# Twenty-four V rows go from VectorE to ScalarE and GpSimd, and the gate round moves from row 84 to row 90

## The chip, the cores and the metric

One core of a Trainium2 chip runs the whole layer. The metric is the device time of one execution in microseconds (us). The kernel is written by hand, engine by engine: TensorE (PE in the profile, PEld its weight loads), VectorE (DVE), ScalarE (ACT), GpSimd (POOL) and the sync engine (SP), each with its own instruction stream, tied to the others by semaphores.

## The reference

Input x is 512 tokens of width 1024, float32. A first sub-layer mixes tokens (a gated MLP group and a retention group, one output projection, LayerNorm). The second is a product-key retrieval over 16384 single-neuron experts, and it is where the change lies:

```python
def _peer(h, w_q, sub_keys, u_tab, v_tab):
    ...
    # 8 heads, 16 experts each: 128 experts for every token
    best_s, best_pos = lax.top_k(cand_s, PEER_TOPK)
    gates = jax.nn.softmax(best_s.astype(jnp.float32), axis=-1)
    ...
    def block(args):
        xt, it, gt = args
        act = jax.nn.gelu(jnp.einsum('td,ted->te', xt, u_tab[it]), approximate=False)
        return jnp.einsum('te,ted->td', gt * act, v_tab[it])
```

So for each token 128 rows of the table U give 128 dot products with h, these go through gelu and are multiplied by the gates, and the 128 rows of the table V with the same indices are summed with these weights. Then follow the residual and the second LayerNorm.

## The kernel before

**Two ways for the experts.** The 512 tokens are four tiles of 128. Tiles 0 and 1 are *gathered*: for each of 8 heads and 16 chosen experts there is one U row and one V row for each of the 128 tokens, fetched by indirect DMA. That is 256 gathered rows in all (tile 0: rows 0 to 127, tile 1: 128 to 255), in the code `n`; `u = n // 16` is the unit (tile and head) whose indices and weights a row uses. One row is a 128x1024 float32 tile, 512 KB. Tiles 2 and 3 are *dense*: TensorE multiplies them with the whole tables, streamed from memory by SP in pairs of blocks of 1 MB (`load_pair`), 64 pairs of U and 64 pairs of V.

**The row loop.** VectorE's stream is one loop over `n` from 0 to 287. At each `n` it does, in this order: the choices of experts due at this `n` (`chosen_before`), the gate round if `n` is `ROUND_ROW`, the one-hots of a *team* of 16 dense tokens if one is due (`team_rows_of`), the product of a dense block with its gates (`gated_gelu`), the dot product of U row `n` (`product_row`, L1177), and the add of V row `n-32` (`add_row`, L1200), which multiplies it by its weight and adds it to the sum of its tile, `acc_rows[t]`. GpSimd's loop has the same `n`: it issues the gather of U row `n` (`gather_u`, L606) and then that of V row `n-32` (`gather_v`, L618). There are six buffers for U rows and six for V rows. So `gather_u(n)` waits until VectorE has done dot product `n-6`, and `gather_v(n)` until V row `n-6` has been added. GpSimd works in order, so a wait of either gather holds the other stream too.

**TensorE's order** is a list (`static_jobs`): first the projections and the mixing, then the queries and key scores up to about 408 us, then the first half of the dense U table in 32 steps (`act`, r = 0; 6.91 us each; ScalarE takes each result from one of four PSUM banks with a gelu), then the *gate round* (32 small groups whose one-hots VectorE and ScalarE make, and whose results VectorE multiplies in), then the first half of V (`expert`, r = 0), in the second half of which the teams (1, 0, m) are interleaved, the second half of U (`act`, r = 1), with the teams (1, 1, m) between its first 16 steps, and the second half of V (`expert`, r = 1).

**What ties the two.** `ROUND_ROW` says at which row VectorE enters the gate round, and the rows of the teams are counted from it: team m of (1, 0) at `ROUND_ROW + 31 + m*15//8`, team m of (1, 1) at `ROUND_ROW + 61 + m*15//8`, the product of block k at `ROUND_ROW + 61 + (k+2)*15//8`. The choices of units 7 to 12 have rows of their own (`LATER_CHOICES`); those of the other gathered units come at `n % 16 == 2`, so that of unit 13 at row 178. At row 160 tile 0 gets its LayerNorm (`finish`).

**The end.** Eleven of the last V rows (229, 231, ..., 249, `TAIL_ROWS`) are added by TensorE, once it has finished the dense experts (`s_vdone`): ScalarE first takes the statistics of tiles 2 and 3 from PSUM, then makes diagonals from the weights (L825). Row 235 can be gathered only when row 229 has been added so. VectorE does the dense statistics at row 264, the dense outputs at row 270, then adds the rows from 240 on and normalises tile 1.

## Time and profile before

| | |
|---|---|
| time, median of 3 runs | 1466.14 us (1464.67 to 1469.86) |
| the profiled execution: its own time | 1468.57 us |
| its span, first to last instruction | 1466.6 us |
| PE busy | 1367.8 us (93%) |
| DVE busy | 1144.3 us (78%) |
| ACT busy | 397.9 us (27%) |
| POOL busy | 663.7 us (45%) |
| TensorE clock granted, mean | 0.975 of full speed |

Busy shares are averages over stages that have different limits, so the stage must be read, not the share. In a timeline a row is one instruction or several equal ones: start, duration, engine, line, operation, tiles, count, and in brackets how long the engine had been idle before it and who ended the wait. `big` holds the gathered rows, `y` the sums. "DMA share" is how busy the 16 DMA engines are on average; about 1.0 with 410 GB/s and more is all that is seen in this trace.

### The profile page before, as it was taken

How to read it: one execution, taken by the hardware profiler on the slowest of the kernel's cores; microseconds unless marked ns; L12 is line 12 of the kernel's file. 1: busy time of each engine (PE TensorE's matmuls, PEld its weight loads, DVE VectorE, ACT ScalarE, POOL GpSimd, SP SyncE). 2: the span in 40 equal slices, each digit the busy share in tenths (PEclk: the TensorE clock that was granted, in tenths of full speed). 3: DMA queues.
4: the chain of work that ended last, by engine and by line, in shares of the span. 5: the costliest groups of instructions: out<-in, count | busy, mean ns of one | idle time of the engine just before them, and what ended most of it. 6: DMA issues, size and time to landing. Idle time of an engine off the chain costs nothing.

```text
span 1466.6 us, 18813 instructions
## 1 busy us (share of the span) xinstructions
PE 1367.8 (93%) x6494; PEld 957.1 (65%) x6494; DVE 1144.3 (78%) x2495; ACT 397.9 (27%) x815; POOL 663.7 (45%) x548
## 2 busy tenths in 40 slices
PE   8999989799999999989999599999999999999943
PEld 6787755488888888867544255578888854444411
DVE  4837266678888888789889998878999887666786
ACT  4224000512120101269410055566551010000020
POOL 2334111353333345620335565645445565666673
PEclk9999999999999999999999799999999999999986
DMA  6411234577878889982599999999899999999996
GB/s 237 151 59 58 91 139 144 187 239 235 314 268 310 291 308 414 414 333 77 185 390 397 401 381 413 403 353 398 336 363 353 414 413 414 414 414 414 412 328 257
DMA packets 118429, 444.26 MB, mean 303 GB/s; under 512 B 11712, under 2 KB 24512, under 8 KB 101952
## 3 DMA queue, kind: packets, MB, share of 16 engines
q0 software_dynamic: 73728, 268.47, 48.1%
q1 hardware_dynamic: 44032, 173.56, 30.9%
q8 instruction: 51, 0.84, 0.2%
q10 hardware_dynamic: 576, 1.05, 0.2%
q14 instruction: 42, 0.34, 0.1%
HBM read 440.94 MB, written 2.10 MB: 302 GB/s over the span
## 4 chain that ended last, share of the span: by engine, by line
DVE 32%; PE 30%; DMA 16%; POOL 7%; issue 6%; DVEq 5%; ACT 4%; ACTq 1%; SPq 0%
DMA big<-in_peer_v_dram,idx 11%; DVE y L1200 8%; PE ps L1441 7%; PE ps L1387 7%; DVE big L1177 7%; PE ps L1370 6%; DMA big<-in_peer_u_dram,idx 4%; POOL big L618 4%; POOL big L606 3%; PE ps L1534 2%; PE ps L1625 2%; DVE work L1060 2%; ACT wr L668 1%; DVE topi L1059 1%; DVE top L1062 1%
## 5 line engine op out<-in xcount | busy, mean ns | idle before, releaser
L606 POOL DMA_INDIRECT big<-in_peer_u_dram,idx x256 | 311.9, 1218 | 537.3 <-DVE dots L1177 430.0
L1177 DVE CUSTOM_DVE_ANT_0 big<-big,xh 128x1024 f32<-128x1024 f32 x256 | 311.7, 1224 | 64.5 <-DMA big<-in_peer_u_dram,idx 42.4
L1200 DVE SCALAR_TENSOR_TENSOR y<-big,wgt,y 128x1024 f32<-128x1024 f32 x245 | 314.1, 1282 | 48.9 <-DMA big<-in_peer_v_dram,idx 45.4
L618 POOL DMA_INDIRECT big<-in_peer_v_dram,idx x256 | 290.7, 1136 | 108.2 <-issue 67.1
L1441 PE MATMUL ps<-big,pool_mem 128*128 128x512 f32 x512 | 224.3, 593 | 0.0
L1370 PE MATMUL ps<-xT,big 128*128 128x256 f32 x960 | 211.1, 380 | 0.0
L1370 PEld LDWEIGHTS ps<-xT,big 128*128 128x128 f32 x960 | 181.7, 190 | 24.3
L1441 PEld LDWEIGHTS ps<-big,pool_mem 128*128 128x128 f32 x512 | 96.7, 190 | 118.6 <-issue 118.6
L1441 PE MATMUL ps<-y,pool_mem 128*128 128x512 f32 x256 | 114.8, 599 | 0.0
L1441 PE MATMUL ps<-xT,pool_mem 128*128 128x512 f32 x256 | 113.5, 593 | 0.0
L1370 PE MATMUL ps<-xT,y 128*128 128x256 f32 x480 | 106.4, 380 | 0.0
L1370 PE MATMUL ps<-xT 128*128 128x256 f32 x480 | 106.4, 380 | 0.0
L1370 PE MATMUL ps<-xT,pool_mem 128*128 128x256 f32 (+1 forms) x512 | 102.4, 360 | 2.7 <-ACTq L760 2.4
L1370 PEld LDWEIGHTS ps<-xT 128*128 128x128 f32 x480 | 90.9, 190 | 12.2
L1370 PEld LDWEIGHTS ps<-xT,y 128*128 128x128 f32 x480 | 90.8, 190 | 12.1
L1370 PEld LDWEIGHTS ps<-xT,pool_mem 128*128 128x128 f32 x512 | 88.0, 194 | 13.3 <-issue 3.4
L482 POOL TENSOR_TENSOR weight_parts<-big,weight_parts 128x1024 fp32r<-128x1024 f32 x20 | 49.1, 2474 | 85.5 <-ACT weight_parts L634 85.4
L1441 PEld LDWEIGHTS ps<-y,pool_mem 128*128 128x128 f32 x256 | 48.8, 192 | 59.5 <-issue 59.1
L1441 PEld LDWEIGHTS ps<-xT,pool_mem 128*128 128x128 f32 x256 | 48.3, 190 | 59.3 <-issue 59.3
L676 ACT ACTIVATE sel<-iota,gated 128x128 f16<-128x128 f32 x256 | 83.7, 553 | 0.1
L1387 PE MATMUL ps<-weight_parts,x_hi 128*128 128x512 f32 x320 | 82.8, 404 | 0.8 <-ACT weight_parts L634 0.8
L634 ACT ACTIVATE pool_mem<-ps 128x512 f32<-128x512 f32 (+2 forms) x52 | 28.5, 549 | 181.3 <-PE ps L1370 86.9
(253 smaller groups left out, 1587.9 us busy)
## 6 DMA issues: line engine op xcount, KB each, us to landing
big<-u_pairs_dram SPq DMA_DIRECT2D x32, 1024.0 KB, 8.0
big<-v_pairs_dram SPq DMA_DIRECT2D x32, 1024.0 KB, 8.0
y<-u_pairs_dram SPq DMA_DIRECT2D x16, 1024.0 KB, 7.9
xT<-u_pairs_dram SPq DMA_DIRECT2D x16, 1024.0 KB, 8.1
y<-v_pairs_dram SPq DMA_DIRECT2D x16, 1024.0 KB, 7.9
xT<-v_pairs_dram SPq DMA_DIRECT2D x16, 1024.0 KB, 8.1
big<-in_w_in_dram SPq DMA_DIRECT2D x24, 512.0 KB, 5.8
pool_mem<-in_peer_w_q_dram SPq DMA_DIRECT2D x12, 1024.0 KB, 7.6
```

The lines of the kernel that those rows point to most:

```text
L482: return engine.tensor_tensor(w_lo(g)[:, ks, :], w_full(g)[:, ks, :], w_hi(g)[:, ks, :].bitcast(f32), ALU.subtract)
L606: nc.gpsimd.indirect_dma_start(urow[n % RING], None, peer_u2, bass.IndirectOffsetOnAxis(ap=idx[:, u, e:e + 1], axis=0)).then_inc(s_u[n % R ...
L618: nc.gpsimd.indirect_dma_start(vrow[n % RING], None, peer_v2, bass.IndirectOffsetOnAxis(ap=idx[:, u, e:e + 1], axis=0)).then_inc(s_v[n % R ...
L676: A.activation(ohl[:, t // 4, :, t % 4], iota[:], ACT.Abs, bias=minus_key[:, c:c + 1])
L1060: V.match_replace(spare, values[:, 0:8], src, NEG)
L1177: V.tensor_tensor_reduce(out=urow[n % RING], in0=urow[n % RING], in1=xh[:, u // PH * D:(u // PH + 1) * D], scale=1.0, scalar=0.0, op0=ALU. ...
L1200: V.scalar_tensor_tensor(acc_rows[t], vrow[n % RING], wgt[:, u % 2, e:e + 1], acc_rows[t], ALU.mult, ALU.add).then_inc(s_vadd, 1)
L1370: last = T.matmul(dst, lhs(i), rhs(i), start=(i == 0), stop=(i == n - 1))
L1387: last = T.matmul(dst, *((a, b_) if x_left else (b_, a)), start=(n == 0 and k == 0), stop=(n == 2 and k == KC - 1))
L1441: last = T.matmul(acc[a][:, half * 512:(half + 1) * 512], X[:, i, a * P:(a + 1) * P], rows_v[:, half * 512:(half + 1) * 512], start=False, ...
L1534: T.matmul(bank, mixT[:, k, t * P:(t + 1) * P], w[:, k, :], start=(k == 0), stop=False)
L1625: last = T.matmul(bank[:, t * QUARTER:(t + 1) * QUARTER], hot[:, t // 4 % 2, :, t % 4], ohi16[:, g % 2, t // 4, c, :, t % 4], start=(c == ...
```

## The change

V rows 0 to 23 leave VectorE. For each of them ScalarE multiplies the gathered row in place by its weight (`weighted`), in its stream just ahead of the evacuation of a dense step given by `weighted_behind`; GpSimd then adds it (`pool_add`) into a sum of their own, which lies in `acc_rows[1]`, not yet in use then. At row 124 VectorE adds that sum to `acc_rows[0]`. ScalarE starts the sum of tile 1 in the same place later, after the fourth step of the second half of U. `ROUND_ROW` becomes 90; with it all rows that are counted from it move by six, while the choice of unit 12 stays at row 174. The gelu of unit 3 and the exponentials of the dense gates come three dense steps earlier on ScalarE.

```diff
-ROUND_ROW = 84
+POOL_ROWS = list(range(24))
+MERGE_ROW = 124
+ROUND_ROW = 90
-LATER_CHOICES = {ROUND_ROW + 1: 7, ROUND_ROW + 6: 8, ROUND_ROW + 12: 9, ROUND_ROW + 18: 10, ROUND_ROW + 24: 11, ROUND_ROW + 90: 12}
+LATER_CHOICES = {ROUND_ROW + 1: 7, ROUND_ROW + 6: 8, ROUND_ROW + 12: 9, ROUND_ROW + 18: 10, ROUND_ROW + 24: 11, ROUND_ROW + 84: 12}
+def weighted_behind(m):
+    return max(0, (4 * m - 9) // 5)
...
+            for m in POOL_ROWS if r == 0 else ():
+                if weighted_behind(m) == n:
+                    jobs.append(("weighted", (m,), None))
             add("act", r, n, by="act" if r == 0 else "dve")
+            if (r, n) == (1, 4):
+                jobs.append(("scale", (1,), None))
...
+            def pool_add(m):
+                if m == 0:
+                    pool.wait_ge(s_h, 2 * GATHERED)
+                    nc.gpsimd.memset(acc_rows[1], 0.0).then_inc(s_pzero, 1)
+                    pool.wait_ge(s_pzero, 1)
+                if m:
+                    pool.wait_ge(s_padd, m)
+                pool.wait_ge(s_weighted, m + 1)
+                nc.gpsimd.tensor_tensor(acc_rows[1], acc_rows[1], vrow[m % RING], ALU.add).then_inc(s_padd, 1)
...
+                elif n - RING in POOL_ROWS:
+                    pool.wait_ge(s_padd, n - RING + 1)
...
                 if n < ROWS:
                     gather_u(n)
+                if n - LAG - RING in POOL_ROWS:
+                    pool_add(n - LAG - RING)
                 if n >= LAG:
                     gather_v(n - LAG)
...
+                if kind == "weighted":
+                    m = arg[0]
+                    act.wait_ge(s_pwgt, m // TOPK + 1)
+                    act.wait_ge(s_v[m % RING], 16 * (1 + m // RING))
+                    A.activation(vrow[m % RING], vrow[m % RING], ACT.Copy,
+                                 scale=wgt[:, m // TOPK, m % TOPK:m % TOPK + 1]).then_inc(s_weighted, 1)
+                    continue
...
+                if n in POOL_ROWS:
+                    return
                 dve.wait_ge(s_v[n % RING], 16 * (1 + n // RING))
...
+                if n == MERGE_ROW:
+                    dve.wait_ge(s_padd, len(POOL_ROWS))
+                    V.tensor_tensor(acc_rows[0], acc_rows[1], acc_rows[0], ALU.add).then_inc(s_merged, 1)
+                    fence()
```

**GpSimd, rows 38 and 39 of the loop.** Before, the engine issues U row 38, V row 6, U row 39, V row 7 and so on, and a V gather waits for VectorE's add (the names in brackets are the semaphores that it waits for):

```order
L606 DMA big<-in_peer_u_dram,idx 128x1024 [waits dots_done]
L618 DMA big<-in_peer_v_dram,idx 128x1024 [waits vrows_added]
L606 DMA big<-in_peer_u_dram,idx 128x1024 [waits dots_done]
L618 DMA big<-in_peer_v_dram,idx 128x1024 [waits vrows_added]
L606 DMA big<-in_peer_u_dram,idx 128x1024 [waits dots_done]
```

In the changed kernel a clearing of the sum and then one add stand between the U gather and the V gather at the same place:

```order
L631 DMA big<-in_peer_u_dram,idx 128x1024 [waits dots_done]
L618 MEMSET y 128x1024 [waits h_ready]
L623 TENSOR_TENSOR y<-y,big 128x1024 [waits vrow_weighted,pool_sum_cleared]
L645 DMA big<-in_peer_v_dram,idx 128x1024 [waits pool_vrows_added]
L631 DMA big<-in_peer_u_dram,idx 128x1024 [waits dots_done]
L623 TENSOR_TENSOR y<-y,big 128x1024 [waits vrow_weighted,pool_vrows_added]
L645 DMA big<-in_peer_v_dram,idx 128x1024 [waits pool_vrows_added]
```

So U row 39 now comes behind the first add, and each U and V row after it, up to row 61 of the loop, behind one more.

**VectorE, the last teams of (1, 1).** Before, the one-hots of team 15 (`ohi`, `wr`) stand at row 173 and the choice of unit 12, which begins with MAX on the scores, at row 174, with no team behind it:

```order
L1231 TENSOR_TENSOR work<-selT,grid 128x512
L1238 TENSOR_TENSOR ohi<-work,pieces 128x1024
L1243 TENSOR_TENSOR wr<-selT,grid 128x1024
L1278 TENSOR_TENSOR pool_mem<-ps,pool_mem 128x512
L1177 ISA big,dots<-big,xh 128x1024
L1177 ISA dots 128x1
L1200 SCALAR_TENSOR_TENSOR y<-big,wgt,y 128x1024
L1057 MAX top<-pool_mem 128x8
```

In the changed kernel the same choice, still at row 174, stands between team 12 and team 13; here is its end, the row's product and add, and team 13:

```order
L1164 TENSOR_TENSOR pick<-work 128x32
L1178 SCALAR_TENSOR_TENSOR idx<-pick 128x16
L1180 TENSOR_SCALAR negmax<-best 128x1
L1215 ISA big,dots<-big,xh 128x1024
L1215 ISA dots 128x1
L1244 SCALAR_TENSOR_TENSOR y<-big,wgt,y 128x1024
L1275 TENSOR_TENSOR work<-selT,grid 128x512
L1282 TENSOR_TENSOR ohi<-work,pieces 128x1024
L1287 TENSOR_TENSOR wr<-selT,grid 128x1024
L1322 TENSOR_TENSOR pool_mem<-ps,pool_mem 128x512
```

The same rows stand once more behind the choice of unit 13 at row 178, ahead of team 15 at row 179: two choices that came after all teams before now come between the last of them.

## Rows read from the trace of the kernel before

**Rows 1.** Stretches of the span: busy time of each engine, granted clock, DMA share, GB/s.

```profile
core 0: us, PE busy (x) PEld busy (x) DVE busy (x) ACT busy (x) POOL busy (x), PEclk, DMA share, GB/s
400.00:540.00 140.00, 139.74 (x667) 123.22 (x666) 122.48 (x400) 20.41 (x35) 44.27 (x39) 1.00 0.80 290
540.00:637.00 97.00, 93.47 (x452) 82.45 (x450) 78.20 (x129) 18.25 (x35) 62.28 (x57) 1.00 1.02 409
...
1178.00:1398.00 220.00, 219.88 (x513) 97.08 (x511) 159.96 (x228) 16.27 (x25) 145.16 (x115) 1.00 1.02 413
```

**Rows 2.** Timeline of PE: start of the gate round, teams 14 and 15, last expert.

```profile
640.69 1.16 PE L1612 MATMUL ps<-ohi,wr 128*128 128x64 f16 x16 [7.22 <-DVEq L1225]
...
1079.00 0.69 PE L1625 MATMUL ps<-ohi,wr 128*128 128x32 f16 x16
...
1087.06 0.69 PE L1625 MATMUL ps<-ohi,wr 128*128 128x32 f16 x16
...
1390.85 7.03 PE L1441 MATMUL ps<-xT,pool_mem 128*128 128x512 f32 x16
```

**Rows 3.** Timeline of VectorE: dot product of row 83, start of the gate round.

```profile
634.43 1.23 DVE L1177 CUSTOM_DVE_ANT_0 big<-big,xh 128x1024 f32<-128x1024 f32 x1 [2.02 <-DMA big<-in_peer_u_dram,idx]
...
637.37 0.29 DVE L1251 CAST pieces<-work 128x256 f16<-128x256 f32 x1
```

**Rows 4.** Timeline of POOL: gathers of U rows 39, 62, 83, V row 57.

```profile
376.81 0.94 POOL L606 DMA_INDIRECT big<-in_peer_u_dram,idx  x1 [0.30 <-issue]
...
541.82 0.94 POOL L606 DMA_INDIRECT big<-in_peer_u_dram,idx  x1 [0.30 <-issue]
...
614.13 1.56 POOL L606 DMA_INDIRECT big<-in_peer_u_dram,idx  x1 [0.30 <-issue]
...
638.39 0.94 POOL L618 DMA_INDIRECT big<-in_peer_v_dram,idx  x1 [0.30 <-issue]
```

**Rows 5.** Timeline of ACT: end of the key scores, and the end of the kernel.

```profile
408.26 0.49 ACT L634 ACTIVATE pool_mem<-ps 128x384 f32<-128x384 f32 x1 [0.18 <-PE ps L1582]
...
1402.59 0.22 ACT L685 ACTIVATE dots<-dots 128x16 f32<-128x16 f32 x1 [48.75 <-DVE dots L1177]
...
1408.08 1.28 ACT L825 ACTIVATE wr<-ident,wgt 128x128 f32<-128x128 f32 x4
```

**Rows 6.** Groups by line: the V adds of VectorE, GpSimd's adds of the early stage.

```profile
L1200 DVE SCALAR_TENSOR_TENSOR y<-big,wgt,y 128x1024 f32<-128x1024 f32 x245 | 314.1, 1282 | 48.9 <-DMA big<-in_peer_v_dram,idx 45.4 <-issue 0.7
L482 POOL TENSOR_TENSOR weight_parts<-big,weight_parts 128x1024 fp32r<-128x1024 f32 x20 | 49.1, 2474 | 85.5 <-ACT weight_parts L634 85.4
```

**Rows 7.** Timeline of POOL: adds of 128x1024 with two inputs, early.

```profile
33.97 4.72 POOL L482 TENSOR_TENSOR weight_parts<-big,weight_parts 128x1024 fp32r<-128x1024 f32 x2 [0.63 <-ACT weight_parts L634]
...
52.95 4.79 POOL L482 TENSOR_TENSOR weight_parts<-big,weight_parts 128x1024 fp32r<-128x1024 f32 x2 [0.68 <-ACT weight_parts L634]
```

**Rows 8.** Timeline of VectorE beside these adds.

```profile
34.31 0.15 DVE L865 TENSOR_SCALAR nw<-mv 128x1 f32<-128x1 f32 x1
...
36.47 2.25 DVE L881 SCALAR_TENSOR_TENSOR nw<-nw 128x1 f32<-128x1 f32 x1
...
55.48 2.81 DVE L897 SCALAR_TENSOR_TENSOR pool_mem<-pool_mem,mv 128x512 f32<-128x512 f32 x1
58.37 0.75 DVE L899 SCALAR_TENSOR_TENSOR pool_mem<-pool_mem,nw 128x512 f32<-128x512 f32 x1
```

**Rows 9.** Timeline of VectorE: teams 14 and 15, choice of unit 12, row 240.

```profile
1073.38 0.68 DVE L1243 TENSOR_TENSOR wr<-selT,grid 128x1024 f16<-128x1024 f16 x1
...
1080.98 0.69 DVE L1243 TENSOR_TENSOR wr<-selT,grid 128x1024 f16<-128x1024 f16 x1
...
1083.53 1.28 DVE L1200 SCALAR_TENSOR_TENSOR y<-big,wgt,y 128x1024 f32<-128x1024 f32 x1
...
1094.56 1.22 DVE L1177 CUSTOM_DVE_ANT_0 big<-big,xh 128x1024 f32<-128x1024 f32 x1
...
1431.35 1.28 DVE L1200 SCALAR_TENSOR_TENSOR y<-big,wgt,y 128x1024 f32<-128x1024 f32 x1 [0.17 <-issue]
```

More of the change, by code:

```diff
@@ L179, in static_jobs @@
         add(kind, *arg, by="dve" if kind == "outA" or kind == "out" and arg[0] < GATHERED else "act")
-    for t in range(GATHERED):
-        jobs.append(("scale", (t,), None))
+    jobs.append(("scale", (0,), None))
     for n in range(PH):
@@ L192, in static_jobs @@
     add("keys", PH - 1, 1, by="act")
-    during = {(0, 2): 1, (0, 12): 2, (0, 26): 3, (1, 4): 8, (1, 11): 9, (1, 20): 10}
+    during = {(0, 2): 1, (0, 12): 2, (0, 23): 3, (1, 4): 8, (1, 11): 9, (1, 20): 10}
     def dense_first_half(r):
@@ L201, in dense_first_half @@
                     jobs.append(("onehot", (1, n + 1), None))
+            for m in POOL_ROWS if r == 0 else ():
+                if weighted_behind(m) == n:
+                    jobs.append(("weighted", (m,), None))
             add("act", r, n, by="act" if r == 0 else "dve")
+            if (r, n) == (1, 4):
+                jobs.append(("scale", (1,), None))
             if (r, n) in during:
                 jobs.append(("gelu", (during[r, n],), None))
-            if (r, n) == (0, 21):
+            if (r, n) == (0, 18):
                 jobs.append(("gates", (), None))
@@ L246, in static_jobs @@
     for i, (kind, arg, by) in enumerate(jobs):
-        if kind in ("split", "norm", "scale", "gelu", "gates", "expert", "onehot", "half", "early", "dnorm"):
+        if kind in ("split", "norm", "scale", "gelu", "gates", "expert", "onehot", "half", "early", "dnorm", "weighted"):
             placed.append((kind, arg, by, None, None))
@@ L458, in layer @@
         s_pv = sem("vrow_in_psum")
+        s_pzero, s_pwgt = sem("pool_sum_cleared"), sem("pool_weights_ready")
+        s_weighted = sem("vrow_weighted")
+        s_padd, s_merged = sem("pool_vrows_added"), sem("pool_sum_merged")
         s_blk = [sem(f"blocks_loaded{s}") for s in range(DPAIRS)]
@@ L615, in gather_v @@
                     pool.wait_ge(s_pv, TAIL_ROWS.index(n - RING) + 1)
+                elif n - RING in POOL_ROWS:
+                    pool.wait_ge(s_padd, n - RING + 1)
                 elif n >= RING:
-                    pool.wait_ge(s_vadd, n - RING + 1 - sum(m < n - RING for m in TAIL_ROWS))
+                    pool.wait_ge(s_vadd, n - RING + 1 - sum(m < n - RING for m in TAIL_ROWS + POOL_ROWS))
                 nc.gpsimd.indirect_dma_start(vrow[n % RING], None, peer_v2,
@@ L647, in _ @@
                     act.wait_ge(s_h, 2 * t + 2)
+                    if t == 1:
+                        act.wait_ge(s_merged, 1)
                     A.activation(acc_rows[t], xh[:, t * D:(t + 1) * D], ACT.Copy, scale=ALPHA).then_inc(s_y, 1)
@@ L1192, in add_row @@
                 t = u // PH
-                if n == 0:
-                    dve.wait_ge(s_y, GATHERED)
                 if e == 0:
+                    if n == PH * TOPK or n == 0:
+                        dve.wait_ge(s_y, t + 1)
+                    if u >= 2 and (u - 2) * TOPK in POOL_ROWS:
+                        dve.wait_ge(s_weighted, min(len(POOL_ROWS), (u - 1) * TOPK))
                     weights(u)
+                    if n in POOL_ROWS:
+                        fence().then_inc(s_pwgt, 1)
                     if u >= GUNITS - 2:
                         fence().then_inc(s_wgt, 1)
+                if n in POOL_ROWS:
+                    return
                 dve.wait_ge(s_v[n % RING], 16 * (1 + n // RING))
@@ L1412, in _ @@
             for kind, arg, by, b, n in JOBS:
-                if kind in ("split", "norm", "scale", "gelu", "gates", "onehot", "half", "dnorm"):
+                if kind in ("split", "norm", "scale", "gelu", "gates", "onehot", "half", "dnorm", "weighted"):
                     continue
```

## The prediction

> **What bounds the kernel now.** I read first the stretches. From 400 to 540 us TensorE is full, VectorE is busy 87% and the DMA engines 0.80; from 540 to 637 the DMA share is 1.02 at 409 GB/s, and VectorE has fallen to 81%: the gathers wait for the memory. It is the same from 1178 to 1398, with TensorE full beside it [rows 1]. Then I looked at where TensorE, which is full nearly everywhere, waits. It waits before the gate round: its first group there starts at 640.69 after 7.22 us of idling [rows 2], because VectorE comes to row 84 only at 637.37, and VectorE had itself waited for the U row 83 [rows 3]. So the round starts when a gather has landed, and everything of TensorE behind it hangs on that start. Last, the end: the dense experts are done at 1397.9 (1390.85 + 7.03) [rows 2], but ScalarE goes on to their statistics only at 1402.6, when the last dot product has freed it, and to the diagonals at 1408.08 [rows 5]. The gathered stream is the later of the two, by some 5 us.
>
> So the time is the start of the round, plus TensorE's work and waits after it, plus a tail behind the last expert. The gathered rows count where they move one of the three.
>
> **The rows before the round.** VectorE loses 24 adds of 1.28 us [rows 6], 30.8 us. GpSimd gets 24 adds. The nearest row is its float32 add of 128x1024 with two inputs, 2.36 to 2.40 us alone (4.72 us for two) [rows 6, 7]. ScalarE gets 24 multiplications of about 1 us, of 20 us in 140 that it is busy [rows 1]; four PSUM banks stand between it and TensorE, so it may be 20 us late before TensorE feels it, and I cost them at nothing.
>
> The first add can't come before the weighted row, and ScalarE has that behind the last key scores, 408.26 + 0.49 us [rows 5], so at about 410. U row 38 is out by then, but U row 39, which went out at 376.81, must now wait behind that add. From there a pass of GpSimd's loop is two gathers of 0.94 us and an add of 2.4 us, each with 0.3 us to the next [rows 4, 7]: 5.2 us. The 24 adds bring it to U row 62 at 410 + 24 x 5.2 = 535 us. Before, that row went out at 541.82 [rows 4]. All that VectorE saves thus buys at most 7 us in the gathers, since GpSimd hands them out in one stream with its adds.
>
> **What the adds take from VectorE.** The trace has GpSimd's adds beside VectorE only in the first stages. There a small VectorE instruction with two SBUF inputs takes 2.25 us, and one of 0.75 us takes 2.81 us, each ending just after GpSimd's add ends; an instruction with one input runs through such an add in 0.15 us [rows 7, 8]. Per add VectorE can lose between nothing and 2.06 us. The dot product has two SBUF inputs; the searches in the choices have one. I take half, 25 us over 24 adds, so of the 30.8 us saved 6 are left, and for GpSimd, which must find the port free too, 5.6 us a pass instead of 5.2. U row 62 then goes out at 410 + 24 x 5.6 = 544, as late as before. Between 5.2 (no loss) and 6.2 us (each of its three steps waits a third of a microsecond) the ends are 535 and 559.
>
> The Trainium skill says as much (Advanced Engine Details and Errata, section GPSIMD Details): the pool engine shares a read and a write interface with VectorE, in conflict with its two-port modes and with instructions that have two SBUF inputs. The rows agree. Taken strictly, every such instruction is shut out for a whole add; in this kernel 24 x 2.4 = 58 us would be lost against 31 saved, U row 62 would go out 27 us later than before, and the sum below would be about 20 us larger. That is a rival below.
>
> **The start of the round.** Before row 90 the dot product of row 89 and the V row 57 are needed, six more of each than before. From U row 62 on the memory is full, and 21 rows took 72.3 us (541.82 to 614.13), 3.44 us each; the dot product of row 83 came 20.3 us after its issue [rows 3, 4]. So row 89 goes out at 544 + 27 x 3.44 = 637 and would be multiplied at 657. SP's blocks stop when TensorE has finished its first half at 633.5 (640.69 - 7.22), so the last gathers have the memory alone: I take off 4 us. VectorE enters the round at 653 instead of 637.4: **+16 us**, with +7 and +30 for the two ends of the pace. It can't be less than -7, because TensorE itself ends its first half only at 633.5.
>
> **The teams behind the round.** The rows are counted from the round, so the dot products and the five choices up to the first team are as before, and so is TensorE's wait there. But the choice of unit 12 stays at row 174 and that of unit 13 at 178, while the last teams move from row 173 to 179. A choice takes 9.7 us (1083.53 + 1.28 to 1094.56) [rows 9]. TensorE takes a team every 8.06 us (1079.00 to 1087.06) and VectorE makes one in 7.6 us (1073.38 to 1080.98) [rows 2, 9]. Team 15 was ready at 1081.67 and wanted at 1087.06: a lead of 5.4 us. The choice at 174 takes 9.7 of that lead, 4.3 us of waiting at team 13; then with no lead left, the choice at 178 costs 9.7 - 0.45 = 9.2 us at team 15. Together **+13 us** on TensorE, between nothing, should VectorE have a lead that the trace of before doesn't show, and 15, since LayerNorm of tile 0 at row 160 falls among the teams as well. The merge at row 124, some 1.3 us, lies in the first teams, where VectorE waits for TensorE.
>
> **The tail.** Six rows are done before the round, so behind it the gathered stream is 6 x 4 us shorter, and with TensorE also later it no longer holds ScalarE at the end: the statistics start with the last expert. The dense statistics and outputs of VectorE then stand right behind. I count from the last expert: 6 us to the diagonals (1402.6 to 1408.1 took 5.5) [rows 5], VectorE's statistics at +6 to +10, its adds up to row 238 to +20 (the V row 238 must be fetched after row 232 has been added), outputs to +25.5, add of row 240 at about +26, against 1431.35 - 1397.9 = 33.5 before [rows 9]. **-7.5 us**. More can't be had from the stream: rows 235 and later wait for TensorE's tail adds.
>
> **The sum.** +16 + 13 - 7.5 = +21.5 us. The profiled execution took 1468.57 us (span 1466.6), so 1490.1; it is 2.4 us above the median of the runs, 1466.14, so the median comes to 1487.6 us. Its own range is 7 + 13 - 7.5 = +12.5 to 30 + 13 - 7.5 = +35.5, that is 1479 to 1502.
>
> **The rivals.**
>
> *VectorE keeps what it saves (faster).* For it speaks that the dot products are a small part of VectorE's work before row 56, where the choices, with one input, fill most of the time; then nothing is lost by sharing, GpSimd's stream is quick, and row 90 is reached before 633.5. The round starts 7 us earlier, the tail gives 7.5, and if the teams' lead also holds, the time is 1466.1 - 14.5 = 1451.6. It decides where start and teams together cost less than 3 us. Against it: GpSimd can't start before 410 and needs 5.2 us a pass. 21%.
>
> *The rows come just late enough (no change).* No loss by sharing, +7 at the round, no wait at the teams, -7.5 in the tail: 1465.6. Against it stands the order of choices and teams, which is certain; for it, that VectorE's lead there is known only from before. 10%.
>
> *Every two-input instruction waits for a whole add.* VectorE and GpSimd hold each other up to row 61, the round starts some 36 us late, and 36 + 13 - 7.5 = +41.5 gives 1508. The 2.81 us row speaks for it; against it, most of the choice instructions have one input. 13%.
>
> *ScalarE holds TensorE.* Its weighted rows wait for V rows; if these come over 20 us late, the four banks run full. It would add to the last case and lies within its price.
>
> **How the numbers follow.** The forecast has 56%, all of it slower by over 0.3% (4.4 us, about what a measurement of this kernel can tell from no change). With the third rival slower is 69%, no change 10%, faster 21%. For 8 in 10 I leave out the top of the third rival and the lower part of the first: 1456 to 1503.
>
> **What the profile after would show.** Right: GpSimd's adds of 2.4 to 3 us from about 410; a dot product or two-input instruction of VectorE up to 2 us longer beside them; U row 62 out at 540 to 560; VectorE's entry to the round near 653, with TensorE idle over 15 us ahead of it; TensorE idle for VectorE twice more among the last teams, 4 and 9 us; the last expert near 1427; ScalarE's statistics right behind it. Wrong: the round entered by 637, or teams 13 and 15 without a wait. The prediction fails most easily at the pace of GpSimd's loop, which I have from two gathers and an add that never stood together.

## The result and the profile after

The changed kernel takes 1510.47 us (median of 4 runs, 1508.15 to 1511.54) against 1465.79 us for the kernel before (1464.67 to 1469.86): ratio 1.0289, 95% interval 1.0271 to 1.0307, 44.7 us slower. The profiled execution took 1508.15 us with a span of 1506.2 us, 39.6 us over the span before; it lies 2.3 us under its median, where the one of before (1468.57) lay 2.8 us above, which is why the spans differ by 5 us less than the medians. I work with the spans. On the chips of the later experiments some executions of a kernel took 20 to 30 us longer than others of the same kernel; the ratios leave these out, the medians don't.

In the changed kernel's lines the dot product is L1215, a V add L1244, GpSimd's add L623, ScalarE's weighting L722, the gate round's matmul L1660, a team's L1673, an expert's L1489. The timeline of PE in the changed kernel: the round, the teams it waits for, the last expert.

```profile
660.47 1.15 PE L1660 MATMUL ps<-ohi,wr 128*128 128x64 f16 x16 [30.16 <-DVEq L1269]
...
859.89 0.69 PE L1673 MATMUL ps<-ohi,wr 128*128 128x32 f16 x16 [17.61 <-DVEq L1288]
...
1045.46 0.69 PE L1673 MATMUL ps<-ohi,wr 128*128 128x32 f16 x16 [10.17 <-DVEq L1288]
...
1106.59 0.69 PE L1673 MATMUL ps<-ohi,wr 128*128 128x32 f16 x16 [2.10 <-DVEq L1288]
...
1131.92 0.69 PE L1673 MATMUL ps<-ohi,wr 128*128 128x32 f16 x16 [8.98 <-DVEq L1288]
...
1437.66 7.03 PE L1489 MATMUL ps<-xT,pool_mem 128*128 128x512 f32 x16
```

Of before only the first team's wait stands beside these (timeline of PE, the kernel before):

```profile
839.51 0.70 PE L1625 MATMUL ps<-ohi,wr 128*128 128x32 f16 x16 [17.52 <-DVEq L1244]
```

With [rows 2] the 39.6 us fall into four pieces. The round starts at 660.47 instead of 640.69: **+19.8**. From there to the first team nothing changes (199.4 against 198.8 us): +0.6. From the first team to the end of the last expert (1444.7 and 1397.9) it is 584.8 against 558.4 us: **+26.4**, where before had no wait at all. Behind the last expert 61.5 us are left instead of 68.7: **-7.2**.

Of the 26.4, the three bracketed waits are 21.25. The rest is TensorE's clock, as the stretches right behind the stop at 1045 show (the columns are those of [rows 1], the changed kernel):

```profile
1046.00:1048.00 2.00, 2.00 (x25) 1.73 (x23) 2.00 (x4) 1.29 (x4) 0.50 (x1) 0.50 0.91 291
1048.00:1050.00 2.00, 2.00 (x6) 1.62 (x5) 1.87 (x4) 1.93 (x8) 1.70 (x2) 0.50 0.41 154
1050.00:1052.00 2.00, 2.00 (x7) 1.61 (x6) 1.48 (x3) 0.94 (x1) 1.53 (x2) 0.61 0.85 248
1052.00:1054.00 2.00, 2.00 (x11) 1.77 (x10) 1.88 (x4) 0.00 (x0) 1.30 (x1) 1.00 0.91 322
```

After the 10 us stop TensorE works at the lower level (0.50, that is 1.2 GHz) to about 1051.6 and then at full speed: 6.1 us at half. Behind the stop that ends at 1131.92 it is the same to about 1136.9, 5.0 us:

```profile
1134.00:1136.00 2.00, 2.00 (x6) 1.65 (x5) 1.87 (x2) 0.00 (x0) 1.71 (x1) 0.50 0.48 190
1136.00:1138.00 2.00, 2.00 (x8) 1.66 (x8) 1.91 (x4) 0.00 (x0) 1.68 (x2) 0.77 0.71 201
```

Half of these 11.1 us is work lost, 5.5 us by this estimate, where 26.4 - 21.25 leaves 5.2. Behind the 2.10 us stop the clock stays at 1.00.

Where does the wait before 1045.46 come from? VectorE's timeline in the changed kernel, at row 160:

```profile
1020.44 1.22 DVE L1215 CUSTOM_DVE_ANT_0 big<-big,xh 128x1024 f32<-128x1024 f32 x1
1021.58 0.08 DVE L1215 DVE_READ_ACCUMULATOR2_ANT dots<- 128x1 f32 x1
1030.63 0.16 DVE L1221 RECIPROCAL rsum<-esum 128x1 f32<-128x1 f32 x1 [8.96 <-ACT best L667]
1032.09 0.23 DVE L1224 SCALAR_TENSOR_TENSOR wgt<-dots,rsum,best 128x16 f32<-128x16 f32 x1 [1.30 <-ACT dots L716]
```

and ScalarE's:

```profile
1027.27 0.58 ACT L838 ACTIVATE ps<-ps 128x512 f32<-128x512 f32 x1 [2.76 <-PE ps L1418]
1027.76 1.05 ACT L679 ACTIVATE y<-xh 128x1024 f32<-128x1024 f32 x1
1028.83 1.28 ACT L667 ACT_TABLE_LOAD   x1
1030.12 0.31 ACT L667 ACTIVATE best<-best,negmax 128x16 f32<-128x16 f32 x1
...
1031.84 0.22 ACT L716 ACTIVATE dots<-dots 128x16 f32<-128x16 f32 x1
```

VectorE is at row 160, where the weights of unit 8 are made. They need ScalarE's exponentials and Gelu of unit 8, which ScalarE has in its list behind TensorE's block (1, 4). That block is only done at 1027. So VectorE, ready at 1021.66, stands 9.0 and then 1.3 us, does the LayerNorm of tile 0 (1033.77 to 1040.83), and TensorE in turn stands 10 us for the team behind that.

Before, the same Gelu was there long ahead of row 160 (timelines of ACT and VectorE, the kernel before):

```profile
1010.33 0.22 ACT L685 ACTIVATE dots<-dots 128x16 f32<-128x16 f32 x1
...
1025.19 0.16 DVE L1183 RECIPROCAL rsum<-esum 128x1 f32<-128x1 f32 x1
```

It was ready 14.6 us before it was wanted. What moved is the place of row 160 among the teams. By `ROUND_ROW + 61 + m*15//8` it is the row of team 8 when the round is at 84 (145 + 15), and the row of team 5 when it is at 90 (151 + 9), while block (1, 4) stays behind team 4. Three teams less at 8.06 us each [rows 2] are 24.2 us; less the 14.6 of before that makes a wait of 9.6 us, an estimate that needs only rows of the kernel before. Measured are 8.96 + 1.30 = 10.3 us with the scale of tile 1 (1.05 us) ahead of the Gelu.

### The profile page after: what moved, and what is told of

It reads as the page before. It is cut to its first block, busy times and chain, and to the rows that moved or that the text cites. A ratio compares the mean times of both kernels' runs of the same rounds, so it can differ in the third digit from the quotient of the medians.

```text
span 1506.2 us, 18870 instructions
## 1 busy us (share of the span) xinstructions
PE 1370.8 (91%) x6494; PEld 960.6 (64%) x6494; DVE 1147.9 (76%) x2472; ACT 422.9 (28%) x839; POOL 717.0 (48%) x573
## 3 DMA queue, kind: packets, MB, share of 16 engines
q10 hardware_dynamic: 576, 1.05, 0.2%
## 4 chain that ended last, share of the span: by engine, by line
PE 43%; DVE 16%; issue 13%; PEld 11%; DMA 5%; ACT 4%; POOL 3%; DVEq 3%; ACTq 1%; PEldq 1%; SPq 0%; POOLq 0%
PE ps L1418 19%; PE ps L1489 7%; PE ps L1435 6%; PEld ps L1489 6%; PEld ps L1418 5%; DVE y L1244 4%; DMA big<-in_peer_v_dram,idx 4%; DVE big L1215 3%; PE ps L1673 2%; PE ps L1582 2%; ACT wr L699 1%; POOL big L645 1%; PE ps L1603 1%; POOL big L631 1%; ACT wr L701 1%
## 5 line engine op out<-in xcount | busy, mean ns | idle before, releaser
L631 POOL DMA_INDIRECT big<-in_peer_u_dram,idx x256 | 307.7, 1202 | 454.8 <-DVE dots L1215 359.3
L1215 DVE CUSTOM_DVE_ANT_0 big<-big,xh 128x1024 f32<-128x1024 f32 x256 | 326.3, 1283 | 64.5 <-DMA big<-in_peer_u_dram,idx 43.2
L1244 DVE SCALAR_TENSOR_TENSOR y<-big,wgt,y 128x1024 f32<-128x1024 f32 x221 | 285.4, 1291 | 63.6 <-DMA big<-in_peer_v_dram,idx 60.9
L1489 PE MATMUL ps<-big,pool_mem 128*128 128x512 f32 x512 | 224.3, 594 | 0.0
L1489 PEld LDWEIGHTS ps<-big,pool_mem 128*128 128x128 f32 x512 | 96.9, 191 | 118.4 <-issue 118.4
L1489 PE MATMUL ps<-y,pool_mem 128*128 128x512 f32 x256 | 115.0, 600 | 0.0
L1489 PE MATMUL ps<-xT,pool_mem 128*128 128x512 f32 x256 | 113.5, 594 | 0.0
L1418 PEld LDWEIGHTS ps<-xT 128*128 128x128 f32 x480 | 92.5, 194 | 12.5
L1489 PEld LDWEIGHTS ps<-y,pool_mem 128*128 128x128 f32 x256 | 49.0, 193 | 59.4 <-issue 59.1
L1489 PEld LDWEIGHTS ps<-xT,pool_mem 128*128 128x128 f32 x256 | 48.5, 191 | 59.2 <-issue 59.2
```

Source lines behind the costliest of these rows:

```text
L631: nc.gpsimd.indirect_dma_start(urow[n % RING], None, peer_u2, bass.IndirectOffsetOnAxis(ap=idx[:, u, e:e + 1], axis=0)).then_inc(s_u[n % R ...
L1215: V.tensor_tensor_reduce(out=urow[n % RING], in0=urow[n % RING], in1=xh[:, u // PH * D:(u // PH + 1) * D], scale=1.0, scalar=0.0, op0=ALU. ...
L1244: V.scalar_tensor_tensor(acc_rows[t], vrow[n % RING], wgt[:, u % 2, e:e + 1], acc_rows[t], ALU.mult, ALU.add).then_inc(s_vadd, 1)
L1418: last = T.matmul(dst, lhs(i), rhs(i), start=(i == 0), stop=(i == n - 1))
L1489: last = T.matmul(acc[a][:, half * 512:(half + 1) * 512], X[:, i, a * P:(a + 1) * P], rows_v[:, half * 512:(half + 1) * 512], start=False, ...
```

## What the adds did beside VectorE

GpSimd's and VectorE's timelines of the changed kernel, two moments:

```profile
428.52 2.36 POOL L623 TENSOR_TENSOR y<-y,big 128x1024 f32<-128x1024 f32 x1
...
459.75 2.36 POOL L623 TENSOR_TENSOR y<-y,big 128x1024 f32<-128x1024 f32 x1
...
547.46 0.94 POOL L631 DMA_INDIRECT big<-in_peer_u_dram,idx  x1 [0.31 <-issue]
```

```profile
428.23 3.75 DVE L1215 CUSTOM_DVE_ANT_0 big<-big,xh 128x1024 f32<-128x1024 f32 x1 [0.20 <-issue]
...
431.90 1.22 DVE L1215 CUSTOM_DVE_ANT_0 big<-big,xh 128x1024 f32<-128x1024 f32 x1
...
459.28 0.27 DVE L1102 FIND_INDEX8 pos<-gated,work 128x8 uint32<-128x112 f32 x1
459.72 2.46 DVE L1133 TENSOR_SCALAR posab<-pos 128x64 uint32<-128x64 uint32 x1 [0.17 <-issue]
```

The dot product that meets the add of 428.52 ends 1.1 us after the add has ended (430.88), so nearly its whole 1.22 us come behind it; the next one takes 1.22. A small one-input TENSOR_SCALAR on integers (0.20 us in the kernel before) stands until the add of 459.75 is over; the searches of the choices (FIND_INDEX8, MAX8, 0.27 to 0.29 us) run through the adds at their usual length. Over 407 to 548 us I added up, for each instruction of VectorE, what it took beyond the usual time of its line and shape: 33 us, of these 15 in the dot products, 10 in TENSOR_TENSOR, 6 in TENSOR_SCALAR. That is all of the 24 x 1.28 = 30.8 us that VectorE saved. The stretch is as full as it was: 121.4 us busy of 138 between 407 and 545, against 121.1 before.

The Trainium skill says it this way (SBUF — State Buffer, section SBUF: two separate sides): the port pair that VectorE and GpSimd share is a lock held for a whole instruction; VectorE takes part in it in its two-port modes, and with two SBUF inputs only against a GpSimd instruction that reads SBUF. By that rule, the trace agrees on the whole instruction (3.75 is about 2.4 + 1.2 us). The page also has the first to start win; here the dot product's row begins 0.29 us ahead of the add's and it waited all the same. At its start GpSimd was still issuing a gather (427.56 to 428.50), so the trace doesn't show which of the two was first by the page's rule.

## The experiments

The first eight ran on one chip, with the kernel before at 1467.6 and 1466.7 us. The later ones fell on other chips, where the kernel before itself took 1494.5 to 1498 us; their ratios are not set beside the first.

**The adds alone: e1_offload_round84.**

```diff
-ROUND_ROW = 90
+ROUND_ROW = 84
-LATER_CHOICES = {..., ROUND_ROW + 84: 12}
+LATER_CHOICES = {..., ROUND_ROW + 90: 12}
```

> The changed kernel with the gate round back at row 84 (and the choice of unit 12 at row 174 as before): the 24 adds on GpSimd alone. Theory A: the adds are a wash, VectorE loses beside them about what it saves, and the 44.7 us come from the round's six rows and from what then falls among the teams. Changed trace: the V add of row 83 ended at about 641.7 us against 637.4 before, so the round is entered 4 us later, no team waits but the first, and the time is about 1470 (1466 to 1475), at most 0.6% over before. Theory B: the sharing of VectorE's port and GpSimd's pace are what makes it slow: then most of the loss stays, 1485 or more, with TensorE idle over 20 us ahead of the round.

1477.36 us, ratio 1.0066 (1.0053 to 1.0080). Timeline of PE and of ScalarE:

```profile
645.46 1.15 PE L1660 MATMUL ps<-ohi,wr 128*128 128x64 f16 x16 [14.69 <-DVEq L1269]
...
844.09 0.69 PE L1673 MATMUL ps<-ohi,wr 128*128 128x32 f16 x16 [17.48 <-DVEq L1288]
```

```profile
1410.39 0.22 ACT L716 ACTIVATE dots<-dots 128x16 f32<-128x16 f32 x1 [49.10 <-DVE dots L1215]
```

Theory A is right on the place (round 4.8 us late, no team waits but the first), but the time is 7 us over its 1470 and outside its range. The whole path is in the second fence: the Gelu behind the last dot product comes at 1410.39 against 1402.59 [rows 5], 7.8 us late, and the span is 8.8 us longer. The adds delay the stream of gathered rows, not only the round.

**The round alone: e2_round90_alone**, the kernel before with the opposite edit of the same two lines.

> The kernel before with the gate round at row 90 (choice of unit 12 at row 174 in both): the round's move alone, no adds on GpSimd. Theory A: the round is entered about 17 us later (six rows at about 3 us), near 655; the row-160 wait of the changed kernel (10 us) comes back in part or whole, since the Gelu of unit 8 stands behind the same TensorE block; the last teams wait 2 and 9 us; the tail gives back 7. Sum about 17 + 21 + 5 (TensorE at half clock after the stops) - 7 = +36, 1502 (1492 to 1510). Theory B: about +10 at most, 1475, since the rows come quicker without GpSimd's adds.

1504.36 us, ratio 1.0253 (1.0238 to 1.0268). Timeline of PE:

```profile
657.68 1.16 PE L1612 MATMUL ps<-ohi,wr 128*128 128x64 f16 x16 [25.10 <-DVEq L1225]
...
1042.66 0.69 PE L1625 MATMUL ps<-ohi,wr 128*128 128x32 f16 x16 [9.54 <-DVEq L1244]
...
1103.02 0.69 PE L1625 MATMUL ps<-ohi,wr 128*128 128x32 f16 x16 [2.14 <-DVEq L1244]
...
1128.62 0.69 PE L1625 MATMUL ps<-ohi,wr 128*128 128x32 f16 x16 [9.25 <-DVEq L1244]
```

Without any of the 24 adds on GpSimd, every team's wait of the changed kernel is there, each within 0.7 us. The round's move makes 37 of the 45 us. It also shows that the wait at row 160 isn't the moved scale of tile 1, which this kernel doesn't move: it is the Gelu of unit 8.

**Unit 8's Gelu earlier: e3_gelu8_early.**

```diff
-    during = {(0, 2): 1, (0, 12): 2, (0, 23): 3, (1, 4): 8, ...}
+    during = {(0, 2): 1, (0, 12): 2, (0, 23): 3, (1, 1): 8, ...}
...
-            if (r, n) == (1, 4):
+            if (r, n) == (1, 1):
                 jobs.append(("scale", (1,), None))
```

> The changed kernel with ScalarE's scale of tile 1 and the Gelu of unit 8 placed behind block (1, 1) instead of (1, 4). In the changed trace VectorE stood 9.0 us at row 160 for this Gelu, which stood behind a TensorE block that came later than VectorE, and TensorE then stood 10.17 us for team 6. Theory A (a wait in a ring: TensorE block, ScalarE's Gelu, VectorE's row 160, TensorE's team): the wait goes, team 6 waits at most for the LayerNorm of tile 0 (7 us less than a lead of 5: 0 to 3 us), and the time falls by 8 to 13 us to about 1499. Rival C: the lead is the same lead that the last teams use, so team 13 and team 15 keep or lower their waits; if the 10 us are given back there or in the gathered stream, the time stays within 4 us of 1510.

1500.84 us, ratio 1.0228 (1.0214 to 1.0241). Timeline of PE, all team waits after the first:

```profile
1101.36 0.68 PE L1673 MATMUL ps<-ohi,wr 128*128 128x32 f16 x16 [4.32 <-DVEq L1288]
...
1126.69 0.69 PE L1673 MATMUL ps<-ohi,wr 128*128 128x32 f16 x16 [6.69 <-DVEq L1288]
```

The wait at row 160 is gone. Its round started at 665.64, 5 us later than the changed kernel's without a reason in the edit, so I count from the round's start to the end: 835.4 us against 845.7, 10.4 less. The last teams wait 11.0 us together as they did (11.1), only split otherwise: team 13 now waits 4.32 us, what the prediction gave it. Behind that stop the clock is at 0.50 for some 6 us, while it stayed at 1.00 behind the 2.10 us of the changed kernel, so a part of what the repair gives is lost again. The time lies 9.6 us below 1510.5, so Rival C (within 4 us) falls.

**Choices behind the teams: e4_choices_behind_teams.**

```diff
-LATER_CHOICES = {..., ROUND_ROW + 84: 12}
+LATER_CHOICES = {..., 180: 12, 183: 13}
```

> The changed kernel with the choices of units 12 and 13 at rows 180 and 183, behind the last team (row 179), instead of 174 and 178. Theory A: the waits of 2.10 and 8.98 us at teams 13 and 15 go, with 3 us of half clock behind the second: 1510 - 14 = 1496 (1494 to 1500); U row 192 is asked for only after product 186, so six rows are left to choose in. Rival D: the gathered stream ends later by what TensorE gains, ScalarE is free only after product 255, and the gain shrinks to under 5 us.

1497.06 us, ratio 1.0204 (1.0190 to 1.0218). No team waits after the one at row 160 (10.17 us, the same as in the changed kernel); from the round's start to the end 832.8 us, 12.9 less. As expected; the gathered stream took no harm (last Gelu at 1419.18, in the changed kernel at 1428.70).

**Both repairs: e5_both_fixes, f1_both_fixes, g1_both_fixes.**

> The changed kernel (round at row 90) with both repairs: scale of tile 1 and Gelu of unit 8 behind block (1, 1), choices of units 12 and 13 at rows 180 and 183. Alone they gave 9.7 and 13.4 us. Theory A: two separate waits among the teams, so the gains add up to 23 us: 1487.5 (1485 to 1490), no wait at a team but the first, and what is left over before is the round's late start (20 us) less the tail. Rival C: both draw on one lead of VectorE over TensorE, so that with one repair the other is partly paid: 1490 to 1495.

> The kernel of e5_both_fixes again, since there the kernel before itself took 1494.5 us and TensorE waited many times for its blocks from memory. Theory A: the two repairs, 9.7 and 13.4 us alone, add up to 23 us: ratio to before 1.0289 - 0.0157 = 1.013 (1487.5 beside 1467). Rival C: both draw on one lead of VectorE, ratio 1.016 to 1.019.

> The kernel of e5_both_fixes a third time, where the kernel before may stand at 1467 us as in the first experiments. If the repairs add up: ratio 1.013, round start near 661, no team waits but the first. If they share one lead: 1.016 to 1.019. If the kernel before again takes 1495 us, TensorE stands in its first half with short gaps for which the trace shows no cause, and the ratio is 0.995 again.

On the other chips: 1487.20, 1494.56 and 1497.15 us, ratios 0.9945, 0.9948 and 0.9913 (0.9922 to 0.9968; 0.9903 to 0.9993; 0.9886 to 0.9939) to a kernel before of 1494.5, 1497.0 and 1498.0. In the profiled execution of e5_both_fixes (span 1483.4) the round starts at 661.52 and only the first team waits (17.64 us); from the start to the end it is 821.9 us, 23.8 less than the changed kernel, where 10.4 and 12.9 add up to 23.3. From the first team to the end of the last expert it is 559.1 us, and 558.4 in the kernel before: the two repairs give back all but 0.7 of the 26.4, the clock's part too. So the two costs are separate, and Rival C falls. The ratio of 1.013 beside a kernel before of 1467 us on the same chip could not be measured; 1.0289 less the two gains of 0.0061 and 0.0085 gives 1.014, and most runs of this kernel took 1483 to 1492 us, 1.2 to 1.8% above 1466. The ratios under 1 don't say that the repaired kernel is the faster one. TensorE has short gaps in its first half on these chips (last section). With the round at row 90 it waits for VectorE there anyway, 30.16 us in the changed kernel and still 13.63 us behind 9.4 us of gaps in e5_both_fixes, so gaps cost this kernel less than one that waits 7.22 us [rows 2].

**The add itself: e6_tiny_adds and e7_fills.** The first cuts GpSimd's add to 32 of 1024 columns in the kernel of e1_offload_round84, the second puts two fills behind each such small add. Both leave most of these 24 rows out of the result. The semaphore increments and the waits between the fills are left out here.

```diff
-nc.gpsimd.tensor_tensor(acc_rows[1], acc_rows[1], vrow[m % RING], ALU.add)...
+nc.gpsimd.tensor_tensor(acc_rows[1][:, 0:32], acc_rows[1][:, 0:32], vrow[m % RING][:, 0:32], ALU.add)...
+for k in range(2):                                   # e7_fills only
+    ...
+    nc.gpsimd.memset(acc_rows[1][:, 32:], 0.0)...
```

> The kernel of e1_offload_round84 (adds on GpSimd, round at row 84) with GpSimd's 24 adds cut to 32 of 1024 columns; the other columns of these 24 rows are left out of the sum. Same instructions and waits, no long add. Theory A (the long adds hold VectorE's two-input instructions and slow GpSimd's passes): the dot products beside them go back from about 1.96 to 1.23 us, U row 62 goes out well before 541.8 us, and the time is at most that of before, 1460 to 1468, against 1477.4 of e1. Rival E (the 35 us that GpSimd stands before the first add, waiting for ScalarE's weighted row, are what the stream loses): U row 62 stays at about 546, and the time stays at 1474 to 1478.

> As e6_tiny_adds, with two fills of 992 columns (about 0.9 us each, one output and no input) behind each small add, so that GpSimd is as busy as with the long adds but reads nothing. If VectorE's loss is GpSimd's reading port, or GpSimd's long pass alone, is told apart: Theory A, sharing: VectorE isn't held, and only GpSimd's pace (about 5.5 us a pass) is left; the time stands between e6 and e1, about 1470. Rival F: what counts is GpSimd's pace alone, whatever it does: then e7 is as slow as e1, 1477, though the dot products are at 1.23 us. If fills hold VectorE as well, dot products over 1.6 us will show it.

1465.32 us, ratio 0.9995 (0.9986 to 1.0004), and 1464.49 us, ratio 0.9981 (0.9973 to 0.9990). The groups of VectorE's dot product between 407 and 545 us in the changed kernel, in e6_tiny_adds and in e7_fills, and GpSimd's fills:

```profile
L1215 DVE CUSTOM_DVE_ANT_0 big<-big,xh 128x1024 f32<-128x1024 f32 x21 | 40.6, 1955 | 5.5 <-DMA big<-in_peer_u_dram,idx 3.5 <-issue 1.4
```

```profile
L1215 DVE CUSTOM_DVE_ANT_0 big<-big,xh 128x1024 f32<-128x1024 f32 x28 | 33.8, 1227 | 12.4 <-DMA big<-in_peer_u_dram,idx 10.0 <-issue 1.4
```

```profile
L1219 DVE CUSTOM_DVE_ANT_0 big<-big,xh 128x1024 f32<-128x1024 f32 x27 | 32.8, 1232 | 18.2 <-DMA big<-in_peer_u_dram,idx 15.8 <-issue 1.4
...
L627 POOL MEMSET y<- 128x992 f32 x48 | 44.5, 927 | 1.4
```

In e7_fills GpSimd is as busy as in e1_offload_round84 (116 of 138 us against 110) and its passes are nearly as long (most 4.5 to 5.5 us against 4.8 to 5.6), but it reads only 32 columns: the dot products keep 1.23 us, and 0.85% of the time goes, 12.5 us. So GpSimd's pace costs nothing measurable and Rival F falls; Theory A's own 1470, which counted that pace, was over 5 us too high. The reading add is the cost. Rival E falls with e6_tiny_adds, where the 35 us that GpSimd stands for the first weighted row are unchanged (35.38) and U row 62 goes out at 521.5 all the same, 20 us before the 541.82 of [rows 4]. The limit of the idea is in these two: were the adds free, the kernel would gain 1 to 3 us by the two ratios. TensorE can then start the round at 630.5 instead of 640.7, and yet the span is only 3.8 us shorter (1462.8). The Gelu behind the last dot product comes 4.9 us earlier (1397.64 against 1402.59) and stands 5.9 us behind the last expert's end (1391.74). The stream of rows ends this kernel, not the round.

**Half as many, and earlier: e8_twelve_rows (POOL_ROWS = list(range(12))) and e10_first_four_early** (weighted rows 0 to 3 placed before the last query and key scores).

> The kernel of e1_offload_round84 with 12 V rows on GpSimd instead of 24. Theory A (what each add gives VectorE it takes back, and GpSimd is slower by the add): half the loss of e1, about 1472. Rival E (the loss is in the start, the 35 us of waiting for the first weighted row): as e1 or nearly, 1476.

> The kernel of e1_offload_round84 with ScalarE's first four weighted rows placed ahead of its last query and key scores instead of behind them, so that GpSimd's first add can start some 20 us earlier (380 to 390 us instead of 407). Rival E: the stream wins what it waited, U row 62 goes out 5 us or more earlier than in e1 and the time falls to 1470. Theory A: the adds only start earlier and then are held by ring and choices as before; U row 56 waits for the choices, not for GpSimd; at most 2 us gained, 1475 to 1477.

1473.19 us, ratio 1.0048 (1.0035 to 1.0061): about 70% of e1's loss for half the adds, though the two intervals barely leave room for a half. VectorE saved 15.4 us and was held for 19.6 (4.2 more), where with 24 adds it saved 30.8 and was held for 32.6 (1.8 more); both kernels start the round at 645.4 to 645.5. And 1473.85 us, ratio 1.0048 (1.0032 to 1.0063): GpSimd's first add at 393.57 instead of 407, U row 62 out at 542.6 instead of 547.9. Theory A allowed this one 2 us and by the ratios it gained 2.6, which the two intervals (each some 2 us wide on either side) can't tell from nothing; a small part of what was lost may be the start. In all round-84 kernels, the copies below included, the span ends 63.5 to 65.2 us behind the last Gelu.

**Copies instead of adds: e12_copies and f2_copies** (`nc.gpsimd.tensor_copy(acc_rows[1], vrow[m % RING])`, which leaves the sum out of the result).

> The kernel of e1_offload_round84 with GpSimd's 24 adds replaced by copies of the weighted row into its sum (one input of 1024 columns, not two; the sum of these rows is left out, only the last stays). It asks whether one long reading input of GpSimd holds VectorE's two-input instructions. If every read of GpSimd from SBUF holds them: dot products beside copies at 1.6 us or more, and a time between e7 (1464.5) and e1 (1477.4). If only two-input instructions of GpSimd do: dot products at 1.23 and a time of 1463 to 1466, as with the fills.

> The kernel of e12_copies again (GpSimd's adds replaced by copies of the weighted row, one input; the sum of these rows is left out, only the last stays). If any long read of GpSimd holds VectorE's two-input instructions, the ratio is 1.002 to 1.007; if only its two-input instructions do, 0.998 to 1.000, as with the fills. In e12_copies the profiled execution spanned 1464.9 us, which speaks for the second, but the runs spread from 1467 to 1502.

On the other chips 1486.76 and 1473.88 us, ratios 0.9835 and 0.9822, spread over 1465 to 1502. Their profiled executions have next to none of TensorE's gaps (three, 0.41 us at most) and the kernel before stood at 1494.5 and 1497.0 there, so the ratios say nothing on the copies. The groups of the two profiled executions do (407 to 545 us):

```profile
L1215 DVE CUSTOM_DVE_ANT_0 big<-big,xh 128x1024 f32<-128x1024 f32 x27 | 36.5, 1367 | 9.6 <-DMA big<-in_peer_u_dram,idx 7.0 <-issue 1.4
```

```profile
L1215 DVE CUSTOM_DVE_ANT_0 big<-big,xh 128x1024 f32<-128x1024 f32 x28 | 39.9, 1443 | 6.0 <-DMA big<-in_peer_u_dram,idx 3.3 <-issue 1.4
```

1.37 and 1.44 us instead of 1.23: a copy, which reads one input (1.03 us alone, 1.13 to 1.14 in the mean), holds the dot product too, by 0.14 to 0.22 us in the mean where the 2.4 us adds hold it by 0.73. Summed as above, the copies held VectorE for 9 and 13 us, the adds for 33. Both expectations put too sharp a line: the size lies between, in the direction that any long read of GpSimd holds.

**Which path ends the kernel: e9_before_round82, f4_before_round82 (round at row 82) and e11_before_round86_fixes, f3_before_round86_fixes, g2_before_round86_fixes (row 86 with both repairs), all from the kernel before.**

> The kernel before with the gate round two rows earlier, at row 82 (choice of unit 12 at row 174 as before). It asks which of two paths ends last: TensorE from the start of the round, or the stream of gathered rows, which has two more rows behind the round. If TensorE is the bound, the round starts some 6 us earlier and the time falls to 1461. If the stream's last product is (it led the end by 65 us in the kernel before and in every kernel with the round at row 84), the two rows cost 4 us each in the memory-bound stretch and give back 6 at the start: 1466 to 1470.

> The kernel of e9_before_round82 again (round two rows earlier, nothing else). TensorE the bound: ratio 0.996. The stream the bound: two rows more behind the round at 4 us each less the 6 us at the start: 1.000 to 1.003.

> The kernel before with the round at row 86 and both repairs, no adds on GpSimd. TensorE's round starts 5 to 6 us later, no team waits but the first, the stream has two rows fewer behind the round and the choices stand behind the teams. If the two ends were balanced before, the time is 1466 to 1469; if the stream alone is the bound, it falls to 1463.

> The kernel of e11_before_round86_fixes again (no adds on GpSimd, round at row 86, both repairs). Ends balanced: ratio 0.999 to 1.002. The stream alone the bound: 0.997. It is the one version here that could beat both kernels.

> The kernel of e11_before_round86_fixes a third time. It had 0.999 and 0.998 beside a kernel before of 1495 us. Where the kernel before takes 1467 us: 0.999 to 1.002 if round start and stream are balanced, 0.997 if only the stream is the bound.

All on the other chips. Row 82: 1503.49 and 1503.70 us, ratios 1.0052 and 1.0051 (1.0031 to 1.0072; 1.0036 to 1.0067), more than either case forecast. The traces show a reason: the round starts at 665.7 and 666.1 without waiting for VectorE, because TensorE's own first half ends late there, so the two rows' 8 us are paid and the 6 us at the start are not given back. Row 86: 1494.14, 1494.57 and 1494.77 us, ratios 0.9990, 0.9983 and 0.9986 (0.9968 to 1.0012; 0.9970 to 0.9996; 0.9972 to 1.0001): 2 us of gain, if any. There too the round doesn't wait for VectorE, so this doesn't say what row 86 would give where the kernel before takes 1467 us. Which path ends last can be read from the last Gelu against the last expert's end: it comes 12.6 and 9.8 us behind it with the round at row 82, 4.7 us in the kernel before on the first chip, and 0.7, -0.2 and -0.3 us with row 86. At 84 the gathered stream is the later end by a little, at 86 the two are level. No version with the whole result was shown to be faster than the kernel before by more than 0.3%, leaving aside the ratios of the repaired kernels above.

## Why the prediction was wrong

It forecast +21.5 us (1487.6 us, own range 1479 to 1502) by the right three places. The change cost 44.7 us by the medians and 39.6 by the spans that the sum is about, outside the range.

- **Start of the round, +16:** +19.8 (660.47; VectorE entered it at 657.2, not 653). The working held in the main: U row 62 forecast for 544 went out at 547.5, holding put at 25 us was 33. The pace was partly luck. Put at 5.6 us a pass because of the shared port, it came to 5.9 in the mean, but from 21 passes of 4.8 to 6.1 us and two of 12.6 and 12.75, in which GpSimd stood over 7 us for VectorE's dot products. e1 and e2 split it: 17.0 by the six rows, 4.8 by the adds, 2 more together than the whole.
- **Teams, +13: the step that failed.** The two waits it named came, 2.1 and 9.0 us (forecast 4.3 and 9.2), but the piece grew by 26.4, beyond even the 15 that it allowed. The prediction compared VectorE's work in each row with TensorE's pace, and took for granted that nothing else that VectorE asks for in those rows is tied to TensorE. It mentioned row 160 only for its LayerNorm. The Gelu of unit 8 is a job of ScalarE placed behind a TensorE block by its number, the row that needs it is placed by the round, and moving the round by six rows put one ahead of the other: 10.2 us of waiting, shown by e2 (9.54 us of it without the adds and without the moved scale) and e3 (10.4 us back by moving this job and the scale). The term could have been had from the kernel before: three teams of 8.06 us against 14.6 us in hand. The same kind of reading, choices against teams, was made for row 174 and not for the rest of the list.
- **The clock, not in the sum at all:** 5.2 us, TensorE at 0.50 behind two of the stops, as shown above.
- **Tail, -7.5:** -7.2. ScalarE's Gelu at 1428.70 comes well ahead of the last expert's end, its statistics start at 1444.77, right behind that end, and VectorE's add of row 240 stands at +27.6 (forecast +26, before +33.5). Here the reason was right.
- **Merge and weightings at nothing:** right; TensorE's waits for ScalarE ahead of the round grew by less than 1 us.
- **The rivals.** "Every two-input instruction waits for a whole add" came nearest in number (1508) by a wrong path, so by luck: it priced a round 36 us late. The dot products show its mechanism, but GpSimd itself was hardly held: its adds took 2.35 to 2.88 us.

What stays open: whether half the adds really cost more than half of the loss, and whether e10's earlier start gains anything. In its trace VectorE was held for 31.8 us, nearly as long as in e1 (32.6), so less holding isn't what it would have gained by.

## What to carry to other kernels

When an item in a hand-made order is moved, list every wait on every engine between its old and its new place, not only those of the engine that bounds. Here ScalarE's Gelu was placed by TensorE's blocks and VectorE's row by the round, so the move closed a ring of waits over three engines, and the time in hand at each such wait (here 14.6 us) says how far the item may move. Before work goes to GpSimd, look at what its reads will hold on VectorE: these 24 adds held it for 33 us and saved it 30.8, while fills that kept GpSimd as busy held it for 3. And before an edit is costed by one path, ask for the other end: here TensorE's start could be had 10 us earlier for only 4 us of time, since the gathered rows ended as late.

## What the runs showed of the hardware that was not expected

- A one-input VectorE instruction can be held by GpSimd's add as well: 2.46 us for a TENSOR_SCALAR of 128x64 on integers that takes 0.20, ending with the add, while searches with one input pass. Beside pure fills the dot products are free (1.23 us), but TENSOR_SCALAR and casts were held there by 3 us in all.
- On the two other chips TensorE's first half has, in most traces, gaps that no semaphore explains. Timeline of PE, f3_before_round86_fixes:

```profile
611.64 0.58 PE L1370 MATMUL ps<-xT,big 128*128 128x256 f32 x1 [2.21 <-issue]
614.45 0.59 PE L1370 MATMUL ps<-xT,big 128*128 128x256 f32 x1 [2.23 <-issue]
617.23 0.59 PE L1370 MATMUL ps<-xT,big 128*128 128x256 f32 x1 [2.20 <-issue]
```

  From 540 to 637 us its PE is busy 72.8 of 97 us at a granted clock of 0.84, with a DMA share of 0.98; in the kernel before on the first chip it is 93.5 at 1.00 [rows 1]. From 1178 to 1398, with the DMA engines just as full, there are none. The chip alone doesn't make them: the profiled executions with copies on these same two chips have PE busy 93.4 of 97 us, and e5_both_fixes 87.6. The cause is open. The kernel before takes 28 us more on these chips; it was not traced there, so that the gaps are the reason is likely but not shown. It makes ratios from different chips incomparable.
